# Two-block transformer kernel: modulation columns interleaved with the output projection's products

## The reference

```
c_act = silu(c)
for l in range(2):
    mod = c_act @ w_ada[l] + b_ada[l]            # 6 x 1024 values
    shift_m, scale_m, gate_m, shift_f, scale_f, gate_f = split(mod, 6)
    h = rms_norm(x, norm_mix[l]) * (1 + scale_m) + shift_m
    x = x + gate_m * hybrid_mixer(h, w_in[l], ..., w_out[l])
    h = rms_norm(x, norm_ffn[l]) * (1 + scale_f) + shift_f
    x = x + gate_f * hierarchical_moe(h, w_router..., w_gate[l], w_up[l], w_down[l])
```

## Time and profile before

| | |
|---|---|
| median of 3 runs | 3231.29 us |
| profiled execution | 3229.41 us |
| its span, first to last instruction | 3227.2 us |
| TensorE busy | 3136.6 us (97%) |
| VectorE busy | 2079.7 us (64%) |
| ScalarE busy | 1357.3 us (42%) |
| mean DMA rate | 190 GB/s |
| mean granted TensorE clock | 0.982 |

### The profile page before, as it was taken

How to read it: one execution, slowest core, us unless ns; L and a number is a source line. 1 busy time by engine, 2 the same in 40 slices (tenths; PEclk the granted TensorE clock), 3 DMA queues, 4 the chain that set the end, 5 groups by cost and what they waited for, 6 DMA issues and landing times.

```text
span 3227.2 us, 46162 instructions
## 1 busy us (share of the span) xinstructions
PE 3136.6 (97%) x15806; PEld 2592.4 (80%) x15806; DVE 2079.7 (64%) x4378; ACT 1357.3 (42%) x2039; POOL 162.5 (5%) x297
## 2 busy tenths in 40 slices
PE   6999999999999999999999999999999999999998
PEld 5688876768887687889888888878788988888887
DVE  5557753545774342899666666665279976666666
ACT  2426642334663243123344444444412334445444
POOL 2100000100000000320000000000032000000000
PEclk8979999999999999999999999999999999999999
DMA  8737887634889632432555555544243255555553
GB/s 296 263 134 287 316 331 302 251 131 153 314 307 347 240 105 74 140 102 80 191 187 189 187 189 188 185 149 146 72 139 105 78 191 190 188 185 191 184 189 122
DMA packets 167141, 614.73 MB, mean 190 GB/s; under 512 B 18752, under 2 KB 18784, under 8 KB 166096
## 3 DMA queue, kind: packets, MB, share of 16 engines
q1 hardware_dynamic: 151632, 551.62, 50.2%
q0 software_dynamic: 15360, 61.16, 5.1%
HBM read 611.66 MB, written 1.05 MB: 190 GB/s over the span
## 4 chain that ended last, share of the span: by engine, by line
PE 86%; DVE 8%; ACT 2%; DMA 1%; DVEq 1%; issue 1%; POOL 0%; ACTq 0%; POOLq 0%
PE PS L1593 13%; PE PS L1595 13%; PE PS L1594 13%; PE PS L2203 11%; PE PS L2204 5%; PE PS L1632 5%; PE PS L2185 4%; PE PS L2166 4%; PE PS L2084 3%; PE PS L1644 2%; PE PS L1886 2%; PE PS L2072 2%; DVE arena L1463 1%; DVE arena L1464 1%; PE PS L1935 1%; DVE arena L1470 1%
## 5 line engine op out<-in xcount | busy, mean ns | idle before, releaser
L2203 PE MATMUL PS<-x_lh,w_hi 128*128 128x512 f32 x1472 | 525.3, 397 | 0.0
L990 DVE TENSOR_TENSOR w_lo<-arena,w_hi 128x1024 fp32r<-128x1024 f32 x440 | 520.9, 1219 | 1.8
L593 ACT ACTIVATE w_hi<-arena 128x1024 fp32r<-128x1024 f32 x440 | 444.0, 1048 | 117.9 <-DMA arena<-in_v_t 79.2
L2204 PE MATMUL PS<-x_lh,w_lo 128*128 128x256 f32 x1472 | 412.8, 280 | 0.0
L1593 PE MATMUL PS<-w_hi,pw_hi 128*128 128x512 f32 x1024 | 406.3, 397 | 6.7 <-DVE w_lo L990 6.2
L1595 PE MATMUL PS<-w_hi,pw_lo 128*128 128x512 f32 x1024 | 402.4, 393 | 0.0
L1594 PE MATMUL PS<-w_lo,pw_hi 128*128 128x512 f32 x1024 | 400.2, 391 | 0.0
L2203 PEld LDWEIGHTS PS<-x_lh,w_hi 128*128 128x128 f32 x1472 | 276.5, 188 | 66.2
L2204 PEld LDWEIGHTS PS<-x_lh,w_lo 128*128 128x128 f32 x1472 | 277.6, 189 | 7.1
L2166 PE MATMUL PS<-x,arena 128*128 128x256 f32 x1024 | 264.3, 380 | 3.9 <-ACT arena L879 3.9
L930 ACT ACTIVATE arena<-PS 128x256 f32<-128x256 f32 x184 | 71.1, 387 | 441.2 <-PE PS L2204 441.2
(11 more groups left out here) (413 smaller groups left out, 5156.1 us busy)
## 6 DMA issues: line engine op xcount, KB each, us to landing
arena<-in_u_t SPq DMA_DIRECT2D x256, 512.0 KB, 4.5
arena<-in_v_t SPq DMA_DIRECT2D x256, 512.0 KB, 3.5
raw<-in_w_gu SPq DMA_DIRECT2D x192, 512.0 KB, 5.3
arena<-in_w SPq DMA_DIRECT2D x152, 512.0 KB, 3.5
arena<-in_w_ada POOLq DMA_DIRECT2D x96, 512.0 KB, 7.3
raw<-in_w_down SPq DMA_DIRECT2D x96, 512.0 KB, 5.4
arena<-in_w_gu SPq DMA_DIRECT2D x64, 512.0 KB, 7.1
arena<-in_w_down SPq DMA_DIRECT2D x32, 512.0 KB, 5.1
```

The source lines that it names most:

```text
L593: A(w_hi[:, m % RING], ring[:, m % RING], ACT.Copy).then_inc(S["hi_done"], 1)
L990: V.tensor_tensor(w_lo[:, m % RING], ring[:, m % RING], w_hi[:, m % RING].bitcast(F32), ALU.subtract)\
L2203: mm(PS[:, 4 + j % 4, :], hi, x_lh[:, :, k], start=k == 0, stop=False)
L2204: last = mm(PS[:, 4 + j % 4, T:2 * T], lo, x_hi[:, k], start=False, stop=k == KT - 1)
```

## The change

The 32 columns of a layer no longer stand ahead of the projection. They stand one by one between the 8 products of each of slots 0 to 3: 8 columns of part 2 with slot 0 (bank 4), the other 24 (parts 3 to 5, bank 5) with slots 1 to 3, what is left of them behind slot 3. In layer 0 the 8 columns of layer 1's part 0 stand with slot 7 (bank 4). VectorE's `ada_mod` is called for part 2 ahead of the first update of x, and for the rest ahead of the third. The count that `ada_mod` waits for is looked up in a list of the 8 calls. Fillers that wrote bank 4 write bank 5.

```diff
+ADA_CALLS = [(0, 1), (0, 2), (0, 3), (0, NMOD), (1, 1), (1, 2), (1, 3), (1, NMOD)]
...
             def ada_mod(l, m0, m1, bank):
                 mod, ga = mods[:, l], gas[:, l]
-                dve.wait_ge(S["ada_ps"], 3 * l + min(m1, 3))
+                dve.wait_ge(S["ada_ps"], ADA_CALLS.index((l, m1)) + 1)
...
-                ada_mod(l, 2, NMOD, 7)
+                ada_mod(l, 2, 3, 4)
                 for j in range(4):
+                    if j == 2:
+                        ada_mod(l, 3, NMOD, 5)
                     dve.wait_ge(S["slot_done"], n0 + W1_IN + 2 * j + 2)
...
-                    ada_mod(1, 0, 2, 5)
+                    ada_mod(1, 0, 2, 4)
...
-            def ada_cols(l, m0, m1, bank):
+            def ada_steps(l, m0, m1, bank):
+
                 pe.wait_ge(S["ada_acc"], 3 * l + min(m1, 3))
                 for j in range(KT * m0, KT * m1):
                     last = mm(PS[:, bank, j:j + 1], ADA["acc"][:, j // KT, P * (j % KT):P * (j % KT) + P], ones[:, 0:1], start=True, stop=True)
-                last.then_inc(S["ada_ps"], 1)
+                    if j == KT * m1 - 1:
+                        last.then_inc(S["ada_ps"], 1)
+                    yield j
+
+            def ada_cols(l, m0, m1, bank):
+                for _ in ada_steps(l, m0, m1, bank):
+                    pass
...
-            def pairs(n0, p0, n, rhs, ready=None):
+            def pairs(n0, p0, n, rhs, ready=None, between=None):
...
                             last = mm(PS[:, (p0 + j) % 4, T * q:T * q + T], ring[:, s % RING, P * k:P * k + P], rhs[:, k],
                                       start=k == 0, stop=k == KT - 1)
+                            if between and k < KT - 1:
+                                next(between.get(2 * j + q, iter(())), None)
                         last.then_inc(S["slot_done"], 1)
+                        if between and between.get(2 * j + q) is not between.get(2 * j + q + 1):
+                            for _ in between.get(2 * j + q, ()):
+                                pass
...
-                ada_cols(l, 2, NMOD, 7)
                 pe.wait_ge(S["outa_ev"], 2 * (l + 1))
                 pe.wait_ge(S["mixb_ok"], l + 1)
-                for j in pairs(n0 + W1_IN, p0 + 8, 4, M["mixT"]):
+                rest = ada_steps(l, 3, NMOD, 5)
+                between = {0: ada_steps(l, 2, 3, 4), 1: rest, 2: rest, 3: rest}
+                if l == 0:
+                    between[7] = ada_steps(1, 0, 1, 4)
+                for j in pairs(n0 + W1_IN, p0 + 8, 4, M["mixT"], between=between):
                     if j:
                         squares(("moe", l), E["sq"], j - 1)
-                if l == 0:
-                    ada_cols(1, 0, 1, 5)
                 squares(("moe", l), E["sq"], 3)
...
-                filler(12, 4)
+                filler(12, 5)
...
-                    ada_cols(1, 1, 2, 5)
-                filler(6, 4)
+                    ada_cols(1, 1, 2, 4)
+                filler(6, 5)
```

## The result

| | before | after |
|---|---|---|
| median of 6 runs each | 3231.56 us | 3248.91 us |
| lowest to highest | 3229.51 to 3233.86 us | 3240.04 to 3250.01 us |
| profiled execution | 3229.41 us | 3248.55 us |
| its span | 3227.2 us | 3246.8 us |
| mean granted TensorE clock | 0.982 | 0.980 |

The account below looks back on a forecast made before the run. TensorE's stream and clock at the mixer's output projection were taken to bound the kernel. Layer 1's +20.3 and layer 0's +18.7 us sum to +39.0 on 3229.4, giving 3268.4; with 1.9 for the median, 3270 us, range 3240 to 3277.

Parts of the forecast that it names:

- Place, and what bounds it: Mixer's output projection, once per layer: TensorE's stream time and clock decide; columns put 6.8 and 7.3 us on the path.
- Price of a product and a column: Slots 0 to 3: product 0.432 us at 2.4 GHz, 0.864 at 1.2; column between products 0.23 or 0.42, its load exposed.
- rival 3: Columns between products: weight loads hidden, columns nearly free; -7 us in each layer, total 3217 us; chance 0.04.
- The wait drops the clock: Ahead of the projection: TensorE idles 3.3 us in both layers and the clock falls to 0.50 as before.
- the 0.7 us that the sum saved in layer 0: Start of layer 0's projection: the first 0.7 us still run at the high clock, saving 0.7 us.
- Does the clock come back among them?: Slots 0 to 3: clock not back before the columns are over; 32 products and 32 columns at 1.2 GHz take 41.1 us.
- rival 2: Clock returns where two products touch, at the ends of slots 1 and 2: about +10 and +9, total 3250 us; chance 0.09.
- the 1.75 us behind slot 3: Products alone behind slot 3: 1.75 us extra for about 3.5 us of them still at the low clock.
- Rival 1: Clock returns within the mixture after some 3.5 us: +0.3 us in layer 1, -0.6 in layer 0, total 3231; chance 0.15.
- Rest of the sum: Behind slot 3: 36 matmuls 15.6 us, layer 0's 7 slot 7 columns 1.6; modulation steps, banks, count, fillers' bank change nothing.
- The first update: VectorE's first update of x was forecast near 181 in layer 0 and 725 in layer 1.
- the 2.6 us that I took as 0: Layer 0's 12 router fillers behind the update: up to 2.6 us could come back if the clock stays up; taken as 0.

Follow-up runs that it names:

- strict alternation: Changed kernel with a column also behind the last product of slots 0 to 3, so no two products touch there: 3269.83 us; repeated unedited, 3266.11 us.
- two and two: Changed kernel with two products, then two columns, in turn through slots 0 to 3: 3235.60 us.
- The small parts alone: Changed kernel with the 32 columns back ahead of the projection, keeping the two modulation steps, banks and slot 7 columns: 3233.82 us, ratio 1.0010 to the kernel before.
- second profile: Profiled execution of the changed kernel run once more, unedited: 3240.90 us; median of that run 3245.80 us.
- one touch: Against strict alternation, in one slot per layer two columns stand behind the third product and none behind the fourth: 3264.16 us.

## Why the prediction was wrong, step by step

- **Place, and what bounds it: right.** 18.5 of the 19.6 us stand in the two projections, on TensorE, at the clock it was granted.
- **Price of a product and a column: right.** Priced 0.864 + 0.42 = 1.28 us at the low clock and 0.432 + 0.23 = 0.66 at the high one; measured 1.28 and 0.66. So a column between two products costs what it costs among its own kind, and rival 3 (3217 us) falls.
- **The wait drops the clock: right.** Forecast 0.7 us after the projection begins in layer 0 and just as it begins in layer 1; in the first profile it fell 0.6 us ahead of it in layer 0 (159.2 against 159.76) and 1.0 ahead in layer 1 (708.7 against 709.68), so the 0.7 us that the sum saved in layer 0 did not come. The kernel with fillers in the wait shows the cause.
- **"Does the clock come back among them?": this step failed.** I took "not before the columns are over", since each return in the rows I had read stood behind products alone. The sum therefore has all 32 products and 32 columns at 1.2 GHz, 41.1 us per layer, where about 23 us did (159.76 to 183.0 and 709.68 to 732.6). I had the two places where products touch before me, named them in the order rows and as rival 2, and gave that 0.09. It is what happened, in both layers and in both profiled executions: slots 0 and 1 at the low clock, the return 1.1 to 3.9 us after the touch at the end of slot 1 began. The experiments narrow rival 2's words: a touch whose column is put beside it brought nothing back in the profiled execution, one with its column left out did. From the first product to the end of the last column is 191.68 + 0.56 - 159.76 = 32.5 us in layer 0, not 41.1 less 0.7, and the 1.75 us behind slot 3 fell away. In layer 1 it is 741.42 + 0.56 - 709.68 = 32.3 us. Rival 2's numbers, +10, +9 and 3250 us, stand against +9.6, +8.9 and 3248.9. The stated range, 3240 to 3277, holds the measured time only because it was drawn wide enough for rival 2; the forecast's own, 3264 to 3277, does not.
- **Why the weight was wrong.** I treated the mixture as one thing with one property. The average over a slot (a third of the time goes to columns) is the same in strict alternation and in two and two, and almost the same in the changed kernel; their stages stand +39, -1 and +18.5 us against before. One column left out of 32 in layer 0's slot 0 moves the stage from 61.4 to 43.0 us.
- **Rival 1 (return within the mixture, 3231 us): its condition was false here** and its price nearly right. With the products in twos the clock does return after 3.4 us, and the two stages together cost -0.8 us where rival 1 had -0.3.
- **Rest of the sum: right, small differences apart.** 36 matmuls at 0.432 behind slot 3 and 7 columns at 0.22 in slot 7 are as priced. The two modulation steps (0.17 us behind a wait of 10.51) are hidden. The small parts alone are 0.1%. Layer 0's ada work made no wait. The first update stands at 180.19, forecast 181; in layer 1 at 730.12, 21.8 us behind the factor, where 725 was forecast and the stage began 4.2 us later. The fillers of the router read 5.49 and 2.94 us, as before. In the second profile layer 0's read 2.94 too; that is the 2.6 us that I took as 0, and it is one of the things by which executions of this kernel differ.

The prediction set a rule of the Trainium skill (TensorE: Matmul & The Clock Gate, Why this matters for your kernels) against its own step: keep TensorE continuously busy to get the full clock. Strict alternation disagrees: 40.80 busy of 40.80 us, clock 0.50. The same table of the Trainium skill advises against idle gaps between bursts of matmuls. The wait here agrees: with 3.3 us without records the clock fell in the changed kernel, and with fillers in them it did not.

Open: why two and two brings the clock back, which leaves no column out, when one touch with its column beside it did not; why the time from the touch to the return varies from 1.1 to 4.2 us; why one execution of strict alternation (3250 us) and two of one touch (3244 and 3258 us) were quicker, of which there is no profile; and the 5 us by which the median of two and two lies above the kernel before.

## What to carry to other kernels

Before you move cheap work out of a wait, read the granted clock behind it. Here the empty wait made the two stages 22.6 us longer than the same kernel with fillers in it. Leaving 14 of the 32 columns in the wait and keeping slot 0 free of them turned the loss into a gain of 9 us; slot 0 free of them alone only made up the loss. Where a stream must start at the low clock, put its wide matmuls first and back to back, and let the single-column ones in once the clock reads 1.00. And where a forecast hangs on a pattern, price the place where the pattern breaks (here a slot's end) as carefully as the pattern.

## What was not expected of the hardware

- TensorE busy without a gap for 40.8 us stayed at 1.2 GHz; the same records with every second column moved by one place got 2.4 GHz after 3.4 us, and with a single column left out 4.2 and 2.2 us after the touch there began.
- The changed kernel's mixture, begun at 2.4 GHz, kept it for 20.7 us (fillers in the wait); begun at 1.2 GHz, the same records stayed there through slots 0 and 1 (19.3 us). Whether the clock is high in these slots therefore depends on what came before them, not only on their records.
- 14 columns in a row at 1.00 (692.4 to 695.7) were enough that it fell behind them; a column and a 128-wide filler in turn over the same 3.2 us were not.
